# Key and output-gate tiles of the mLSTM projection as pairs of seven block products

## The reference

```
cx = silu(c)
sh1, sc1, g1, sh2, sc2, g2 = split(cx @ ada_w + ada_b, 6)       # adaLN
hx = modulate(rmsnorm_2(x, pre_mix_g), sh1, sc1)                # 1024 x 1024
p = hx @ m_in_w + m_in_b                                        # 1024 x 3088
q, k, v, o, gates = split(p, [512, 1024, 2048, 3072], axis=-1)  # 4 heads
...
y = (hn * sigmoid(o)).astype(o.dtype)                           # readout
```

## Time and profile before

| | |
|---|---|
| Median of 3 runs | 2078.43 us (2077.24 to 2079.9) |
| Profiled execution: span from first to last instruction | 2076.5 us; the runs above take 0.7 to 3.4 us more |
| TensorE busy | 2014.3 us (97%) |
| VectorE busy | 1223.6 us (59%) |
| ScalarE busy | 819.1 us (39%) |
| GpSimd busy | 989.1 us (48%) |
| DMA | 251.42 MB, 121 GB/s on average |

### The profile page before, as it was taken

The page is one execution under the profiler, slowest core; times in us unless marked ns, Lnnn a source line. Parts: engine busy times, 40 slices in busy tenths (PEclk is TensorE's granted clock), DMA queues, the critical chain, the costliest instruction groups (busy, mean ns, idle before and its releaser), DMA issues.

```text
span 2076.5 us, 24039 instructions
## 1 busy us (share of the span) xinstructions
PE 2014.3 (97%) x9167; PEld 1663.5 (80%) x9167; DVE 1223.6 (59%) x1276; ACT 819.1 (39%) x1066; POOL 989.1 (48%) x560
## 2 busy tenths in 40 slices
PE   6999999999999999999999999988999999999999
PEld 5788888888788888878887888766788888878877
DVE  6889998877642475545502565589655555523125
ACT  5343355566452323221123464445344334412135
POOL 1376655555222222123311446648877877722244
PEclk7999999999999999999999999999999999999999
DMA  9641122122112323448855865341222222253123
GB/s 377 216 142 41 54 63 63 56 68 74 41 61 81 121 83 101 146 115 283 278 161 160 279 230 163 93 151 61 62 61 61 80 83 87 66 193 125 46 89 127
DMA packets 269263, 251.42 MB, mean 121 GB/s; under 512 B 8330, under 2 KB 230291, under 8 KB 269155
## 3 DMA queue, kind: packets, MB, share of 16 engines
q1 hardware_dynamic: 266067, 238.42, 36.3%
q10 hardware_dynamic: 3088, 11.54, 1.4%
HBM read 206.08 MB, written 43.84 MB: 120 GB/s over the span
## 4 chain that ended last, share of the span: by engine, by line
PE 51%; issue 14%; POOL 6%; DVE 1%; DMA 1%; ACT 0%; POOLq 0%; SPq 0%; DVEq 0%; ACTq 0%
PE PS L2227 16%; PE PS L1739 16%; PE PS L2005 5%; PE PS L2119 5%; POOL wl L851 3%; PE PS L2241 1%; PE PS L2063 1%; PE PS L2064 1%; PE PS L2072 1%; POOL SCR L1042 1%; PE PS L1928 1%; PE PS L2052 1%; PE PS L2153 1%; POOL wl L1029 1%; POOL XL L1025 0%
## 5 line engine op out<-in xcount | busy, mean ns | idle before, releaser
L851 POOL TENSOR_TENSOR wl<-raw,wh 128x1024 fp32r<-128x1024 f32 (+1 forms) x157 | 377.6, 2406 | 807.9 <-ACT wh L1098 589.7
L1739 PE MATMUL PS<-XH,wh 128*128 128x512 f32 x1424 | 442.4, 392 | 7.2 <-POOL wl L851 3.0
L1739 PE MATMUL PS<-XH,wl 128*128 128x512 f32 x1424 | 441.1, 391 | 0.0
L1739 PE MATMUL PS<-XL,wh 128*128 128x512 f32 x1424 | 440.6, 391 | 0.0
L1739 PEld LDWEIGHTS PS<-XH,wh 128*128 128x128 f32 x1424 | 264.9, 188 | 64.0 <-POOL wl L851 4.0
L1739 PEld LDWEIGHTS PS<-XL,wh 128*128 128x128 f32 x1424 | 265.7, 188 | 54.1
L1739 PEld LDWEIGHTS PS<-XH,wl 128*128 128x128 f32 x1424 | 265.4, 188 | 53.5
L1098 ACT ACTIVATE wh<-raw 128x1024 fp32r<-128x1024 f32 (+1 forms) x108 | 111.0, 1028 | 436.9 <-PE PS L1739 187.2
L2470 DVE SCALAR_TENSOR_TENSOR PS<-B,PJ,PS 128x1022 f32<-128x1022 f32 (+7 forms) x197 | 251.1, 1275 | 7.5
L1171 ACT ACTIVATE wh<-raw 128x1024 fp32r<-128x1024 f32 x48 | 50.8, 1058 | 248.2 <-PE PS L1739 228.7
L1029 POOL TENSOR_TENSOR wl<-SCR,wh 128x512 fp32r<-128x512 f32 x80 | 114.2, 1429 | 69.7 <-ACT wh L1567 69.1
(11 more groups left out here) (439 smaller groups left out, 3747.8 us busy)
## 6 DMA issues: line engine op xcount, KB each, us to landing
B<-in_ada_w SPq DMA_DIRECT2D x48, 512.0 KB, 5.4
raw<-in_ffn_up_w SPq DMA_DIRECT2D x48, 512.0 KB, 4.1
raw<-in_w_in SPq DMA_DIRECT2D x40, 512.0 KB, 4.5
raw<-in_m_in_w SPq DMA_DIRECT2D x37, 512.0 KB, 5.0
mod_tiles<-in_mod_w SPq DMA_DIRECT2D x16, 512.0 KB, 13.2
raw<-in_w_out SPq DMA_DIRECT2D x16, 512.0 KB, 5.0
qkvo_d<-B SPq DMA_DIRECT2D x16, 512.0 KB, 3.5
raw<-in_m_out_w SPq DMA_DIRECT2D x16, 512.0 KB, 4.2
```

The lines of the kernel that those rows point to most:

```text
L851: tt(wl[slot][:, 0:kc, :], raw[slot][:, 0:kc, :], wh[slot][:, 0:kc, :].bitcast(F32), ALU.subtract).then_inc(lo_done, 1)
L1739: last = mm(ps[:, c:c + step_n], W[:, k, :], Y[:, k, c:c + step_n], start=(seen == 0), stop=(seen == total - 1))
```

## The change

- The order of the stage is now: gate tile, four query tiles, value product, then six pairs (`O_PAIRS`): two of keys, four of output gates. Each pair is seven products (`o_product`) of 12 matmuls.
- Weights: `pair_load` loads both raw tiles of a pair; `o_high` on ScalarE, `o_low` and `o_weight_sum` (four a pair) on GpSimd. `pair_load(s + 1)` waits until the four weight sums of pair s are made, and stands ahead of the adaLN loads of pair s in SyncE's queue.
- Tokens: three combinations of four blocks each. `token_sum` on VectorE (28 instructions of 128 x 512), `token_high` on ScalarE (12), `token_low` on GpSimd (12), all within the value product, and a fourth operand that is put in place of a quarter of XH and XL after it: `t3_sum` (12 on GpSimd), 4 highs on ScalarE, `t3_low` (4 on VectorE). Product 6 of pair 0 waits for the last.
- Banks: `o_copy` on ScalarE and `bank_sum_pair` on VectorE, seven a pair, write the two staging rows. Product n of a pair waits until the bank that it takes, used eight products before, has been read. The first bank sum of a pair waits until both staging rows of the pair before are stored. ScalarE evicts (`o_finish`) and issues the stores itself.
- adaLN: of 32 `late_sums` four stay in the value product, 28 stand one behind each bank sum of pairs 0 to 3. The first matmuls of pair 4 (the ten transposes) wait for all 32. The narrow matmuls go into pair 4.
- Gate rows: the reversal copies and `rows_sb` now come behind the evictions of the value product's first pass, and `rows_store` with its wait behind the load of the eighth unit of that product.
- The load of the weight units six and seven moves ahead of the store of the forget gates. Context chunks load half of the broadcast rows. The first recurrence step has the last bank sums of pair 5 beside it.

```diff
+    O_PAIRS = (HQ // P + KD) // 2
...
-        late_t = [b2[:, n * D:(n + 1) * D] for n in range(4)]
+        late_t = [SCR[:, n:n + D] for n in (512, 2048, 3588, 5124)]
...
+        def o_bank(q):
+            b = (q + (2 if q >= 7 * (O_PAIRS - 2) else 0)) % 8
+            return part(PS[b // 2], b % 2)
...
@@ SyncE @@
+            for u in range(4, V_UNITS):
+                proj_unit(V_FIRST + u)
+                if u in (6, 10, 14):
+                    v_store((u - 6) // 4)
+                if u == 7:
                     rows_store()
                     sp.wait_ge(*at("rows_out", 16 * 10))
+                if u == V_UNITS - 1:
+                    for n in range(4):
+                        late_load(n)
+
+            def pair_load(s):
+                for v in range(2):
+                    if s == 0:
+                        sp.wait_ge(lo_done, PAIR_UNIT + 1 + v)
+                    else:
+                        sp.wait_ge(*at("oq_lo", 7 * s - 5 + v))
+                        sp.wait_ge(*at("os_ok", 4 * s))
...
+            pair_load(0)
+            v_store(3)
+            for s in range(O_PAIRS):
+                pair_load(s + 1)
...
+                if s < O_PAIRS - 2:
+                    for n in range(4 + 7 * s, 4 + 7 * (s + 1)):
+                        late_load(n)
...
@@ GpSimd @@
+            T3_AT = {0: (0, 2), 1: (2, 4), 2: (4, 6), 3: (6, 8), 4: (8, 9), 14: (9, 12)}
+            LOW_AT = {7: (0, 2), 9: (2, 4), 10: (4, 6), 11: (6, 8), 12: (8, 10), 13: (10, 12)}
...
+            for q in range(7 * O_PAIRS):
+                o_low(q)
+                s, i = divmod(q, 7)
+                if 1 <= q <= 4:
+                    o_weight_sum(0, q - 1)
+                elif 6 <= q <= 9:
+                    o_weight_sum(1, q - 6)
+                elif i in (5, 6) and 0 < s < O_PAIRS - 1:
+                    for n in range(2 * i - 10, 2 * i - 8):
+                        o_weight_sum(s + 1, n)
...
@@ ScalarE @@
+            def o_copy(s):
+                act.wait_ge(*at("oq_used", 7 * s + 1))
+                if s:
+                    act.wait_ge(*at("osum_ok", SUMS * s))
+                f(US[:], o_bank(7 * s), ACT.Copy).then_inc(ev("opair_copy"), 1)
...
+            for s in range(O_PAIRS):
+                o_high(7 * s + 4)
+                o_copy(s)
+                if s:
+                    o_finish(s - 1, 1)
...
@@ TensorE @@
+            def o_product(s, i):
+                q, (W_H, W_L) = 7 * s + i, (ring(wh, 7 * s + i), ring(wl, 7 * s + i))
...
+                    if n == 0:
+                        pe.wait_ge(*at("opair_copy", before + 1))
+                    else:
+                        pe.wait_ge(*at("osum_ok", SUMS * before + (0, 1, 7, 6, 2, 4, 5)[n]))
...
+                elif s == 0 and i == 6:
+                    pe.wait_ge(*at("t3_lo", HK))
+                for k in range(HK):
+                    for n, (W, Y) in enumerate(((W_H, X_H), (W_L, X_H), (W_H, X_L))):
+                        ins = mm(bank, W[:, k, :], Y[:, k, :], start=(k == 0 and n == 0), stop=(k == HK - 1 and n == 2))
...
+            for s in range(O_PAIRS):
+                if s == O_PAIRS - 2:
+                    pe.wait_ge(*at("gate_rows_in", 16))
+                    pe.wait_ge(*at("opair_copy", s))
+                    pe.wait_ge(*at("late_summed", LATE * KD))
...
@@ VectorE @@
+            def bank_sum_pair(s, n):
+                i = (1, 4, 3, 5, 6, 3, 2)[n]
+                dve.wait_ge(*at("oq_used", 7 * s + max(i, (1, 4, 4, 5, 6, 6, 6)[n]) + 1))
+                if n == 0:
+                    dve.wait_ge(*at("opair_copy", s + 1))
+                    dve.wait_ge(*at("proj_out0", 16 * (DIRECT[0] + s)))
+                    dve.wait_ge(*at("proj_out1", 16 * (DIRECT[1] + s)))
...
+            v_evac(0)
+            for q in range(5):
+                reverse(UN[q], RQ[q])
+            dve.sem_inc(ev("rows_sb"), 1)
...
+            for s in range(O_PAIRS):
+                for n in range(SUMS if s < O_PAIRS - 1 else 5):
+                    bank_sum_pair(s, n)
+                    if s == 0 and n < 2:
+                        t3_low(2 * n)
+                        t3_low(2 * n + 1)
+                    if s < O_PAIRS - 2:
+                        late_sums(4 + 7 * s + n, 5 + 7 * s + n)
+                    elif s == O_PAIRS - 2 and n == 3:
+                        last_rows()
+                    elif s == O_PAIRS - 1 and n == 1:
+                        zero_state()
```

391 lines of the change are left out of this document (262 added, 129 removed).

## The result

| | before | after |
|---|---|---|
| median of 4 runs each, us | 2077.84 (2077.22 to 2079.9) | 2110.03 (2107.3 to 2114.43) |
| ratio, 95% interval | | 1.0151, 1.0132 to 1.0171 |
| span of the profiled execution, us | 2076.5 | 2112.4 |
| end of the query tiles (880.4 before, 878.1 after) to the recurrence's second four transposes (1131.3, 1164.7), us | 250.9 | 286.6 |
| from there to the end of the span, us | 945.2 | 947.7 |

The change costs 32 us; 12 were forecast. The spans differ by 35.9: the stage is 35.7 longer, what follows 2.5, and the kernel came to the stage 2.3 earlier. Before the change the key tiles follow the query tiles, after it the value product does.

The account below looks back on a forecast made before the run. TensorE's matmuls were taken to bound the stage. -16.3 - 1.4 + 5.4 + 1.7 + 19.9 + 1.7 + 1 = +12.0 us on the profiled 2076.5, plus 1.9 from span to median, gave 2090.4 us, range 2072 to 2104.

Parts of the forecast that it names:

- What is removed: Key and gate tiles: 576 matmuls become 504, -16.3 us; a 1.4 us weight-tile wait goes too.
- Step 1: Value product: gate-row stores delay the ninth unit's load, with GpSimd contention; +5.4 us, plus 1.7 for the clock.
- Step 2: Pair 0: product 6 waits 3.5 us for low parts queued on VectorE behind adaLN tile 4's sum.
- Step 3: Pairs 0 to 3: VectorE's chain makes cycles 20 to 22 us; with pair 0's wait +19.9, some 13 before pair 4.
- The clock: Lower granted clock after TensorE idles: +1.7 us in the value product and +1.7 behind the wait before pair 4.
- What stays covered: ScalarE, GpSimd's direct sums, VectorE's token sums and DMA at 275 GB/s fit beside the matmuls, adding no time.
- The tail: First context step finds extra bank sums beside it, while context chunks load less: +1 us, ends -2 and +3.
- Rival A: Pairs: GpSimd and VectorE's shared SBUF lock is the bound, 23.0 us of work in 19.04; 2100 us, chance 0.2.
- Rival B: Pairs: VectorE keeps pace if the handoff at a pair's start is under 3.8 us; 2079 us, no change, chance 0.2.

Follow-up runs that it names:

- e15: Changed kernel with nine of GpSimd's direct sums moved into the last two query tiles: 2106.83 us, ratio 1.0117.
- e8: e7 with GpSimd's direct sums, SyncE's row-store wait, two token sums and pair 0's adaLN sums moved later: 2090.77 us, ratio 1.0043.
- e10: e7 with the 32 one-column products interleaved with products 3 to 5 of pair 4 instead of 1 to 3: 2095.98 us, ratio 1.0071.
- e13: Changed kernel with e15's table, e10's waits and columns, weight sums on VectorE, adaLN sums 10 in value product, then 5, 5, 5, 4, 3: 2079.2 us, ratio 0.9986.
- e12: Changed kernel with e15's table, e10's waits and columns, ten adaLN sums in the value product, weight sums left on GpSimd: 2085.53 us, ratio 1.0021.
- e14: e13 with the weight sums left on GpSimd: 2080.78 us, ratio 0.9995.
- e6: Changed kernel with VectorE's wait for the second staging tile's store moved from the pair's first bank sum to bank sum 5: 2107.77 us, ratio 1.0121.
- e7: e6 plus TensorE's wait for all adaLN sums split, before the first column of each group in pair 4: 2095.73 us, ratio 1.0066.
- e17: e13 with value pass 2's evictions before the last three token sums, ScalarE's highs over units 9 to 13, last direct sums in unit 15: 2080.14 us, ratio 0.9993.

## Why the prediction was wrong

The side was right (slower, 0.68), the size was not: 2090.4 us, 2072 to 2104, measured 2110.03.

- **What is removed** stands: 72 matmuls fewer. Without idle time and half clock the stage is 233.7 us in the changed kernel (286.6 - 40.0 - 12.9) and 248.5 before, 14.8 less where 16.3 was forecast.
- **Step 1** failed. It put 5.4 us at the ninth unit, where 1.1 us was measured. The waits are for VectorE's evictions: 7.4 behind the gate rows and 5.0 behind six token sums, with 1.8 for GpSimd 14.2 us in all. The chain that the step did describe was there: the ninth unit's load was issued at 935.0 behind the row stores, and the unit was ready at 943.0, 10.5 us after it would have been due (932.5). Only 1.1 shows because the wait of 7.4 and the half clock behind it had made TensorE late by then. The term mis-sized is "I add 2 us" for contention with nine more sums: it was 8.9 (e15). The step let the gate rows end at 904.0 "as before", where they ended at 914.15, and followed a delay through one queue, SyncE's; that pass 1 waits for the banks of pass 0, and so for whatever stands on VectorE before their evictions, was not in it. The second wait was not foreseen at all, and it isn't in every profile.
- **Step 2** held: 3.5 forecast, 4.4 measured, at the place and behind the instructions named. In e8, where the adaLN sums stand behind the low parts, it is gone.
- **Step 3** had the right mechanism, VectorE's chain through the pairs, and one wrong term, the time behind a store. The wait before pair 4 was 13.1 us (some 13 forecast) and the others 3.4 and 3.7 (0.3, 1.2, 2.0). That the 13 came out is luck: counted from the end of the value product, VectorE's last adaLN sum ended after 107.5 us (96.1 forecast) and product 6 of pair 3 after 94.5 (83.2 with the forecast's waits), both some 11 late. The store was taken at the 3.5 us of the earlier trace rows, which no adaLN load ran beside; it took 8.1. "Were it slower, each store adds to step 3" was said, and no number was put on it, though 275 GB/s was worked out in the same paragraph. From the last bank sum of a pair to the first of the next it took 10.2 to 11.8 us (5.8 and 7.0 forecast), so a cycle was 24 us instead of 20 to 22. adaLN sums took 1.56 us on average, not 1.66. The 0.8 for those that only multiply had no row behind it; they took 1.05. Three adaLN sums do stand behind bank sums that need product 6, but these were late anyway: bank sum 4 ran at 1107.7, product 6 had ended at 1101.1.
- **The clock** was the other large miss: 1.7 + 1.7 forecast, 12.9 measured. The forecast took its price once a step; each of the six waits of 3.4 us or more had it, and in e10 and e13 some of 2.0 to 2.9 too; the same wait of 2.2 us in e12 and e14 had none.
- **What stays covered**: ScalarE and GpSimd's work in the pairs held. VectorE's token sums did not (the 5.0 us), and DMA did not, as above: 230 GB/s were moved, not 275.
- **The tail**: +1 forecast, +2.5 measured.
- **Rival A** was not the bound here: adaLN sums took under 2 us on average, and in the pairs TensorE never waited for GpSimd, though its other sign was there (GpSimd busy for 74% of 1012 to 1100 us, two thirds forecast). But its mechanism is under the others. When the queue orders were mended (e8), waits for GpSimd's weight parts took their place, and the time was 0.4% over before. The rival had the wrong payer, GpSimd's operations and not VectorE's.
- **Rival B** would have been the kernel without the store wait; e6 and e7 show that this alone doesn't give it.

## What to carry to other kernels

When work is moved beside a product, add up what each pair of engines that take turns must do in one cycle, as well as looking at each wait: mending queue orders alone brought this kernel from 1.5% slower to 0.4% (e8), and the versions that came level (e13, e14, e17) also have less adaLN work in a pair. A wait is set by everything that stands before the awaited instruction in its queue, and by when that queue could start, not by the length of the one instruction: with sums over 8 columns 9.4 of 13.1 us were left, because the series began behind a store. Price a transfer with the traffic that the change itself brings, and add a price for the clock to every wait.
